# A score product issued once more, ahead of the product that waits for a copy, in the attention stage of a hybrid decoder layer

## The reference, cut to what matters

```
hn = rmsnorm(h, g_mix_pre);  z = hn @ w_in          # q, k, v, indexer q/k/w, pool input
score = sum_h w[t,h] * relu(q_idx[t,h] . k_idx[s])  # causal; the 256 best keys of each query are kept
s  = (q . k) * HEAD_DIM**-0.5, -inf where not kept
pr = softmax(s);  o = pr @ v                        # 8 query heads, 2 key/value heads, width 64
mix = concat(o, pool_mixer) @ w_o;  h = h + rmsnorm(mix)
m = square(relu(rmsnorm(h) @ w_up)) @ w_down;  h = h + rmsnorm(m)
h = h + rmsnorm(sigmoid(h @ w_ple_gate) * (p @ w_ple_proj))
```

## Time and profile before

| | |
|---|---|
| median of 3 runs | 3409.25 us (3407.23 to 3410.01) |
| the profiled execution's own time | 3407.94 us |
| its span, first to last instruction | 3406.1 us |
| PE busy | 3075.7 us, 90% of the span |
| DVE, ACT, POOL busy | 1694.6, 1332.1, 328.1 us |
| mean granted TensorE clock | 0.940 of 2.4 GHz |

### The profile page before, as it was taken

How to read it: one execution, slowest core, us unless ns; L and a number is a source line. 1 busy time by engine, 2 the same in 40 slices (tenths; PEclk the granted TensorE clock), 3 DMA queues, 4 the chain that set the end, 5 groups by cost and what they waited for, 6 DMA issues and landing times.

```text
span 3406.1 us, 37933 instructions
## 1 busy us (share of the span) xinstructions
PE 3075.7 (90%) x13944; PEld 2364.1 (69%) x13944; DVE 1694.6 (50%) x3385; ACT 1332.1 (39%) x2162; POOL 328.1 (10%) x421
## 2 busy tenths in 40 slices
PE   5998887788887888997899999999999999999998
PEld 4776765566666666785688856888668886588873
DVE  3376767677876767731333343333433334333333
ACT  3253436566756557653323222322222223232221
POOL 1332320213030130000000000000000000000000
PEclk9998987888997888998999999999999999999999
DMA  3111122221110110101633312323213323132310
GB/s 121 55 46 51 41 84 71 57 57 44 37 50 27 44 34 20 53 30 50 231 99 97 119 51 75 117 94 99 87 57 124 99 87 105 50 121 90 99 50 25
DMA packets 215452, 250.88 MB, mean 74 GB/s; under 512 B 57952, under 2 KB 160096, under 8 KB 215264
## 3 DMA queue, kind: packets, MB, share of 16 engines
q1 hardware_dynamic: 212960, 239.99, 22.2%
q10 hardware_dynamic: 2304, 8.39, 0.6%
HBM read 208.34 MB, written 40.01 MB: 73 GB/s over the span
## 4 chain that ended last, share of the span: by engine, by line
issue 60%; PE 23%; DVE 8%; ACT 5%; POOL 2%; DMA 1%; SPq 0%; DVEq 0%; POOLq 0%; ACTq 0%
PE bank L1673 6%; PE bank L1653 5%; PE bank L1538 5%; PE bank L1556 2%; PE bank L1639 2%; PE bank L1557 2%; ACT kept L895 1%; DVE kept L1199 1%; ACT score_tail L895 1%; POOL score L816 1%; DVE too_few L1207 1%; ACT probsT L983 1%; DVE probs L1328 1%; POOL rstdC L840 1%; DVE threshold L1216 1%
## 5 line engine op out<-in xcount | busy, mean ns | idle before, releaser
L1403 DVE TENSOR_TENSOR w_lo<-w_raw,w_hi 128x1024 fp32r<-128x1024 f32 x256 | 312.6, 1222 | 517.5 <-ACT w_hi L1026 511.3
L1026 ACT CAST w_hi<-w_raw 128x1024 fp32r<-128x1024 f32 x256 | 267.3, 1045 | 561.7 <-PE bank L1538 535.1
L1653 PE MATMUL bank<-values,probsT 128*128 128x64 f32 x2176 | 333.2, 300 | 144.8 <-ACT probsT L983 120.8
L1653 PEld LDWEIGHTS bank<-values,probsT 128*128 128x128 f32 x2176 | 312.1, 218 | 171.5 <-ACT probsT L983 159.4
L1538 PE MATMUL bank<-hn_hi,w_hi 128*128 128x512 f32 x1024 | 399.8, 390 | 14.5 <-DVE hn_lo L1420 10.8
L1538 PE MATMUL bank<-w_hi,hid_lo 128*128 128x512 f32 x1024 | 405.9, 396 | 0.0
L1538 PE MATMUL bank<-w_lo,hid_hi 128*128 128x512 f32 x1024 | 405.9, 396 | 0.0
L1538 PE MATMUL bank<-w_hi,hid_hi 128*128 128x512 f32 x1024 | 405.9, 396 | 0.0
L1538 PE MATMUL bank<-hn_lo,w_hi 128*128 128x512 f32 x1024 | 399.2, 390 | 0.0
L1538 PE MATMUL bank<-hn_hi,w_lo 128*128 128x512 f32 x1024 | 399.2, 390 | 0.0
L1328 DVE CUSTOM_DVE_ANT_0 probs<-bank,mask 128x384 f32<-128x384 f32 (+3 forms) x320 | 193.9, 607 | 248.1 <-PE bank L1557 247.4
(11 more groups left out here) (191 smaller groups left out, 4798.2 us busy)
## 6 DMA issues: line engine op xcount, KB each, us to landing
w_raw<-in_w_up SPq DMA_DIRECT2D x64, 1024.0 KB, 5.6
w_raw<-in_w_down SPq DMA_DIRECT2D x64, 1024.0 KB, 5.1
x_in<-in_x SPq DMA_DIRECT2D x16, 512.0 KB, 3.8
q_t<-q_scratch SPq DMA_DIRECT2D x32, 256.0 KB, 3.6
x_t<-in_x SPq DMA_DIRECT2D x16, 512.0 KB, 4.4
h_scratch<-h_t SPq DMA_DIRECT2D x16, 512.0 KB, 2.9
hnT_scratch<-hn2T_t SPq DMA_DIRECT2D x16, 512.0 KB, 3.9
hn_lo<-hnT_scratch SPq DMA_DIRECT2D x4, 2048.0 KB, 11.2
```

The lines of the kernel that those rows point to most:

```text
L1026: nc.scalar.copy(w_hi[:, p % 4, :].rearrange("p (k f) -> p k f", f=piece_width(p)), raw_piece(p)).then_inc(w_hi_rdy, 1)
L1403: nc.vector.tensor_tensor(out_p, raw_piece(p), hi_p.bitcast(F32), ALU.subtract).then_inc(w_lo_rdy, 1)
L1653: last = nc.tensor.matmul(bank[:, 4, h * HEAD:(h + 1) * HEAD], probsT[:, m % 3, a * P:(a + 1) * P], values[:, kt, HEAD * kv:HEAD * (kv + 1 ...
```

## The change

Ahead of `weigh(m)` PE now issues the first of the two products of the first score block of step m + 1, into the bank where that block will be computed, once the ring has released it. Nothing reads this result: in step m + 1 the same product starts the bank anew (`start=True`), and the second one adds to it. It is left out where the next block is the first of a tile (its queries may not be there yet), where step m + 1 has no score block, and in the steps that hold work of the indexer, whose banks would come first in the ring. No other engine's order changes.

```diff
+            def rehearse(blocks_next):
+                for H, b in blocks_next[:1]:
+                    i, h = divmod(H, Q_HEADS)
+                    o, w = blocks[i][b]
+                    if (h, b) != (0, 0):
+                        wait_ring(("s", H, b))
+                        nc.tensor.matmul(bank[:, ring_bank[("s", H, b)], 0:w], q_hi[:, i % 2, h, :],
+                                         k_parts[:, h // (Q_HEADS // KV_HEADS), o:o + w], start=True, stop=True)
...
+                if m + 1 < len(steps) and not at["turn"].get(EARLY_SPOTS + m) and not at["index"].get(EARLY_SPOTS + m):
+                    rehearse(score_at[m + 1])
                 weigh(m)
```

## The result

The changed kernel takes 3415.59 us (median of 20 executions, 3407.13 to 3422.68) against 3408.66 us of the kernel before (20 executions, 3407.23 to 3410.23). The ratio is 1.0018, with a 95% interval of 1.0012 to 1.0024: 6.9 us slower, a small loss that is clear of noise. The forecast was 3415 us.

What follows compares the result with a forecast made beforehand. PE alone was taken to bound the kernel after 1400 us; before, a circle of ACT, PE and DVE with PE sometimes at low clock. 3407.94 + 16 + 14 - 23 = 3414.9, so 3415 us, range 3387 to 3433.

Steps and rivals of the forecast that it cites:

- The tail: After 1400 us, behind the search: 71 added products, all on the path, cost 16.0 us; 24 with weight load exposed.
- The clock: 650 to 1400 us: added work in PE's idle stretches removes a third of 228 us at low clock, gaining 23 us.
- The net ahead of the tail: Before 1400 us: 14 us path cost from 106 of 185 products not meeting a copy wait, less 23 us clock gain.
- The ring: Before each added product, PE's wait for DVE to release the bank: costed at 0, under 2 us in all.
- The waits: In the search, PE's weighing waits for ACT's copy, 120.6 us in all, should shrink by some 15 us.
- The range of A: The forecast case, a third of the low clock goes: 3415 us, own range 3406 to 3422, chance 0.42.
- B: Ahead of the tail, the drops to low clock stay and the kernel is clearly slower: 3430 to 3438 us, chance 0.24.
- C: Ahead of the tail, most drops go, two thirds of the low time: 3389 us, 3383 at three quarters, chance 0.28.
- D: Before 1400 us, later copy waits take up the lag, so the 106 products cost nothing: 3401 us, chance 0.06.

Runs made afterwards that it cites:

- e2: The changed kernel with only the 63 added products behind the threshold search kept: 3422.64 us, +14.0 us against the kernel before.
- e1: The changed kernel with added products only in the 244 steps holding the threshold search, 193 of 256: 3402.35 us, -6.3 us against the kernel before.
- e3: The same 193 products as e1, issued right behind the weighing product instead of ahead of it: 3401.56 us, -7.1 us against the kernel before.
- e4: As e1, with each added product issued twice, 386 in all: 3387.46 us, -21.2 us against the kernel before.
- e11: As e4, with the pair behind the weighing product: 3405.28 us, ratio 0.9985 to 1.0003 against the kernel before.
- e7: As e4, with three or four transposes of the values in place of the two products: 3386.70 us, -22.6 us against the kernel before.

## Why the prediction was right

The forecast was 3415 us, the median is 3415.59. The mechanism, a cost in full behind the search and a partial gain by the clock ahead of it, is what the runs show. That the number fits to 1 us is in part luck, as the two terms ahead of the tail show.

- *The tail.* 16.0 us were worked out for 71 products, from the time between the starts of L1557 and its successor. The traces have 15.9 us between steps 236 and 319, and e2 has 14.0 us for 63. That the weight load takes the place of one already exposed fits: with it exposed the forecast had 24 us.
- *The clock.* A third of the low-clock time was to go; 30% went (228 to 160 us). The clock was forecast at 0.92 and 0.88 and is 0.92 and 0.87. This share was an estimate without a row behind it, so that it came out is luck. e1, with the same products ahead of the tail, has 174 us in its profile; over all executions the two save nearly the same (63 and 61 us in the whole kernel).
- *The net ahead of the tail.* 14 - 23 = -9 us was forecast. It is -9.0 us by the medians, -10.8 in the profiled execution, and e1 has -6.3 (2.7 to 9.2 us won by its interval). No run measures the two terms apart. With 0.27 us of time for each us of low clock, where the prediction had 0.46 x 0.65 = 0.30, the 63 us saved give 17 us, and 8 us are left for the cost. By this estimate both terms were some 6 us too large, and they cancel.
- *The ring.* Costed at 0; one wait of 1.1 us. The reading behind it was too narrow: the 0.2 + 0.2 us of the earlier trace rows are two of the rows in which L1556 waits for DVE. The same view also has its waits for L1186, 8.7 us in 15 and 2.9 us in 2, behind the indexer's work. As the rehearsals leave out the steps with such work, it did no harm.
- *The waits.* "Some 15 us less" of 120.6; 14.5 less. It proves little, as e3, with its products behind the waits, has 11.5 less.
- *The range of A.* Its own inputs, a path share of a third to two thirds of 28 us and a gain of 15 to 32 us, give 3407.94 + 16 + 9 - 32 = 3401 to 3407.94 + 16 + 19 - 15 = 3428 us, and not 3406 to 3422. The median lies in both.
- *Rivals.* B (the drops stay) and C (most go) are both refuted for this dose. C's mechanism is real and needs two products: e4 has 57% of the low clock gone and wins 21 us. D (the added work is hidden too) has its number, 3401 us, refuted; its mechanism is in part there, since e3's rows show a wait taking such a lag up, and the cost left for the 185 products is below the forecast's 14 us. e11 shows that such work costs when it lies between the weighing and the score.
- *What was not seen.* The prediction argued that the gain comes from filling waits. For the clock the place made little difference: 61 us less of low clock ahead and 70 behind with one product (e1, e3), 138 and 114 with two (e4, e11).

## What to carry to other kernels

In this kernel, work added to keep TensorE's clock up paid only in the stretches where the granted clock was below 1 and the engine waited; where PE was busy throughout at clock 1.00, every added product was paid in full. So look for such stretches first. Place the work inside the wait, raise the dose until the time stops falling (here two products per step), and look at the time, not at the mean clock: the clock kept rising from 0.960 over 0.965 to 0.969 while the time rose from 3387 to 3399 us. The best version here needs one condition and one loop more than the change as it was made, and turns a loss of 6.9 us into a gain of 21.2.

## What the runs showed that I had not expected

- Float32 transposes hold the clock as well as products of about the same duration (e7: 3386.70 us, e4: 3387.46 us).
- With one product a step the executions of one kernel spread far more than before: 3407.13 to 3422.68 us, against 3407.23 to 3410.23. With two, ahead of the weighing, they are close again (3386.34 to 3388.51), and with two behind it they spread (3399.00 to 3413.74). The clocks on record say where it comes from: the slow executions are those with more time at the low clock (0.947 against 0.953 in the result above). Drops that are close to being avoided, and so fall out differently from one execution to the next, would explain that; which drops differ was not traced.
